# A one-core decoder layer with 32 experts: PSUM pairs released after the first reader, 1/rms by one-hot products, the last expert's weights in quarters

## Time and profile before

| | |
|---|---|
| runs shown | 824.47, 823.37, 822.83 us; median 823.37 |
| the profiled execution | 825.39 us, span 823.57 us |
| mean granted TensorE clock | 0.991 of full speed |
| busy | PE 721.8 us, DVE 288.8, ACT 179.6, POOL 102.6 |
| moved by DMA | 258.39 MB, mean 314 GB/s |

### The profile page before, as it was taken

One profiled execution on the slowest core, in us unless ns is written; L12 is line 12 of the kernel. 1 busy time (PEld: TensorE's weight loads), 2 busy tenths in 40 slices (PEclk: granted clock), 3 DMA queues, 4 the chain that ended last, 5 costly groups with the idle time before them and its releaser, 6 DMA issues.

```text
span 823.6 us, 11299 instructions
## 1 busy us (share of the span) xinstructions
PE 721.8 (88%) x4520; PEld 450.1 (55%) x4520; DVE 288.8 (35%) x520; ACT 179.6 (22%) x274; POOL 102.6 (12%) x161
## 2 busy tenths in 40 slices
PE   8999999999999888999998887777777777778996
PEld 8989999899998433333333222222222222226775
DVE  5556788676434532010111011011001001005875
ACT  7242312233323010011111010000000000004576
POOL 0500000010001112212121211211211111100000
PEclk9999999999999999999999999999999999999999
DMA  9641225663936799999999999999999999995301
GB/s 347 239 181 53 77 80 210 248 224 98 400 132 217 259 409 416 428 426 425 426 425 426 424 427 427 426 425 428 428 424 429 426 427 426 425 422 218 120 27 77
DMA packets 36457, 258.39 MB, mean 314 GB/s; under 512 B 7905, under 2 KB 8465, under 8 KB 22841
## 3 DMA queue, kind: packets, MB, share of 16 engines
q1 hardware_dynamic: 27248, 237.17, 70.3%
q0 software_dynamic: 7072, 19.07, 6.2%
q10 hardware_dynamic: 2096, 1.56, 0.6%
HBM read 251.04 MB, written 15.14 MB: 323 GB/s over the span
## 4 chain that ended last, share of the span: by engine, by line
PE 53%; DMA 36%; DVE 6%; ACT 3%; issue 2%; SPq 0%; DVEq 0%; POOLq 0%; ACTq 0%
DMA arena<-in_w_exp 33%; PE ps L1560 23%; PE ps L1754 15%; PE ps L1771 5%; PE ps L1885 3%; PE ps L1603 1%; DMA region_q<-in_xt 1%; DVE xh L1423 1%; DVE region_u L1376 1%; DMA region_u<-h_rows,index 1%; DMA region_m<-y_rows 1%; PE ps L1568 1%; DMA y_rows<-region_v,both_cols 1%; PE ps L1762 1%; PE ps L1673 0%
## 5 line engine op out<-in xcount | busy, mean ns | idle before, releaser
L1754 PE MATMUL ps<-arena,region_u 128*64 128x512 f32 x960 | 218.3, 600 | 47.0 <-DMA arena<-in_w_exp 46.0
L1754 PEld LDWEIGHTS ps<-arena,region_u 128*64 128x64 f32 x960 | 66.9, 137 | 196.2 <-issue 124.2
L1372 DVE SCALAR_TENSOR_TENSOR region_u<-ps,small,region_u 128x256 f32<-128x256 f32 x32 | 15.5, 484 | 376.7 <-ACT region_u L858 376.7
L1560 PE MATMUL ps<-u_hi,w_hi 128*128 128x260 f32 x448 | 129.2, 288 | 5.1 <-issue 3.3
L1560 PE MATMUL ps<-u_lo,w_hi 128*128 128x260 f32 x448 | 127.4, 284 | 0.0
L1560 PE MATMUL ps<-u_hi,w_low 128*128 128x260 f32 x448 | 127.3, 284 | 0.0
L1771 PE MATMUL ps<-arena,region_u 128*64 128x512 f32 x480 | 109.6, 598 | 6.1 <-DMA arena<-in_w_exp 2.5
L1560 PEld LDWEIGHTS ps<-u_hi,w_hi 128*128 128x128 f32 x448 | 85.1, 190 | 7.0 <-issue 5.0
L1560 PEld LDWEIGHTS ps<-u_hi,w_low 128*128 128x128 f32 x448 | 85.2, 190 | 0.0
L1560 PEld LDWEIGHTS ps<-u_lo,w_hi 128*128 128x128 f32 x448 | 85.2, 190 | 0.0
L682 POOL DMA_INDIRECT y_rows<-region_v,both_cols x32 | 33.3, 1042 | 367.6 <-ACT region_v L862 367.6
(11 more groups left out here) (288 smaller groups left out, 857.6 us busy)
## 6 DMA issues: line engine op xcount, KB each, us to landing
arena<-in_w_exp SPq DMA_DIRECT2D x88, 2048.0 KB, 26.9
arena<-in_w_in SPq DMA_DIRECT2D x35, 512.0 KB, 4.0
region_q<-in_w_exp SPq DMA_DIRECT2D x24, 256.0 KB, 11.1
arena<-in_w_exp SPq DMA_DIRECT2D x8, 512.0 KB, 4.2
arena<-in_w_ple_gate SPq DMA_DIRECT2D x2, 2048.0 KB, 23.6
region_u<-in_xt SPq DMA_DIRECT2D x2, 1040.0 KB, 6.2
arena<-in_state_ret POOLq DMA_DIRECT2D x2, 1024.0 KB, 9.1
xh<-v_few POOLq DMA_DIRECT2D x1, 2048.0 KB, 9.0
```

Source lines behind the costliest of these rows:

```text
L1372: V.scalar_tensor_tensor(hs[b], ps[:, 2 + b, 256:512], rs[b], sg[b], ALU.mult, ALU.mult).then_inc(out_sem, 1)
L1560: last = mm(halves(out)[:, half, :], w[:, k, :], u[:, cols], start=(k == 0 and s == 0), stop=(k == KD - 1 and s == 2))
L1754: last = mm(ps[side * 64:side * 64 + 64, 2 + b, :], xv[:, k // 4, k % 4, :], rows(k % 4 * 2 + side), start=(k == 0), stop=(k == KD - 1))
```

## The change

Four things, in the order of the kernel.

1. *Head.* DVE counts a q or k job as read after its first operation; a new semaphore `rotated` counts the sums, and PE's sc, DVE's far product, `state_row`, the mask of q3 and ACT's reuse of `rot` wait for it. ot's pair is read by ACT in place of DVE, right before the squares.
2. *Router.* `h_rows` has rows of 512 words; 1/rms goes into its own `r_rows`, which ACT stores after the first two experts and which only the branch for overfull experts gathers. For the others a new job rs makes a table on chip: DVE multiplies `pick` with 1/rms (one operation on 128x320), ACT widens the row one-hots to float32 (128x640), PE does 20 float32 products, DVE copies 32 columns. `evac_rows` reads the table. 16 spins after tot become 6 after rs.
3. *Weights.* Spare 1: its first two pieces are issued after POOL's first memset of a gather tile, the other two after `h_rows`. Spare 2 is issued when POOL has issued the first gather. For the last pair of experts SP's loop is written out; units 94 and 95 come in four DMAs each, with a semaphore for each quarter, and PE waits for them one by one.
4. *Tail.* 52 spins for 48, and 8 more before u of turn 1; DVE's order as below.

```diff
-READERS = dict(... ot="D" ...)
+READERS = dict(... ot="A" ..., rs="D")
+    jobs += [("rk", 0), ("ix", 0), ("iy", 0), ("tot", 0), ("rs", 0)]
-SPIN_TAIL = 48
+SPIN_TAIL, SPIN_ROWS = 52, 8
-HR = 528
-SPIN = (28, 8, 16)
+RW = 16
+SPIN = (28, 8, 6)
@@ SP
+            sp.wait_ge(xg_cleared, 1)
+            for n in range(2):
+                load_spare(1, n)
             sp.wait_ge(h_stored, 16 * 2 * len(STORES))
-            for n in range(4):
+            for n in range(2, 4):
                 load_spare(1, n)
-            sp.wait_ge(xg_loaded[0], 16)
+            sp.wait_ge(pool_turn, 2)
             for n in range(8):
                 load_spare(2, n)
...
-            with sp.Fori(4, NE // 2) as i:
+            with sp.Fori(4, NE // 2 - 1) as i:
...
+            for j in range(6):
+                unit, slot = NE * 3 - 6 + j, PAIR_SLOTS[j]
+                sp.wait_ge(used[j % 3], NE - 2 + (j // 3 - 1))
+                if j < 4:
+                    load_unit(unit, slot)
+                for n in range(PIECES if j >= 4 else 0):
+                    at = slice(n * PIECE, n * PIECE + PIECE)
+                    sp.dma_start(ring[:, slot, at], a["w_exp"][unit][:, at]).then_inc(last_loaded[j - 4][n], 16)
@@ POOL: the wait for rstd_stored moves into the branch for overfull experts
@@ ACT
-                        act.wait_ge(dve_jobs, HEAD.done("D", ROTATED[turn - 2]))
+                        act.wait_ge(rotated, turn - 1)
...
+                elif kind == "ot":
+                    nc.scalar.activation(qk[:, 0:H, SEQ:T], b[:, 0:H * NB].rearrange("p (h n) -> p h n", h=H),
+                                         ACT.Copy).then_inc(act_jobs, 1)
+                    act.wait_ge(act_jobs, done)
+                    for h in range(H):
+                        nc.scalar.activation(qk[:, H + h, :], qk[:, h, :], ACT.Square).then_inc(o_squared, 1)
...
-            act.wait_ge(rows_ready, 1)
-            for half in range(2):
-                act.dma_start(h_full[:, :, half, 512:HR], rstd_rows[:, 0:4, :]).then_inc(rstd_stored, 16)
-                act.dma_start(h_few[:, half, 512:HR], rstd_rows[0:NB, 4, :]).then_inc(rstd_stored, 16)
+            act.wait_ge(hot_done, 1)
+            nc.scalar.activation(hot_32, row_hot, ACT.Copy).then_inc(hot_widened, 1)
@@ ACT, after pair_of_experts(0)
+            act.wait_ge(rows_ready, 1)
+            for half in range(2):
+                act.dma_start(r_full[:, :, half, :], rstd_rows[:, 0:4, :]).then_inc(rstd_stored, 16)
+                act.dma_start(r_end[:, half, :], rstd_rows[0:NB, 4, :]).then_inc(rstd_stored, 16)
@@ DVE, q and k
-                    link(V.tensor_tensor(dst..., halves(b), cos_t..., ALU.mult))
+                    V.tensor_tensor(dst..., halves(b), cos_t..., ALU.mult).then_inc(dve_jobs, 1)
                     link(V.tensor_tensor(r, r, sin_t, ALU.mult))
-                    V.tensor_tensor(dst, dst, r, ALU.add).then_inc(dve_jobs, 1)
+                    dve.wait_ge(dve_jobs, done)
+                    V.tensor_tensor(dst, dst, r, ALU.add).then_inc(rotated, 1)
@@ DVE, rk and rs
+                    V.tensor_tensor(rs_value..., pick, stats[:, 10:15]..., ALU.mult).then_inc(value_ready, 1)
+                elif kind == "rs":
+                    V.tensor_copy(rs_table, b[:, 0:NE]).then_inc(dve_jobs, 1)
-                V.tensor_copy(rs[b], xg[b][:, 512:513])
+                V.tensor_copy(rs[b], rg[:, 0:1] if over else rs_table[:, bass.ds(count - 1, 1)])
@@ DVE, tail
-            combine(1, 1)
             gained(0)
+            combine(1, 1)
             gained(1)
...
                 if n + 1 < NT:
                     gained(n + 1)
-                    if n + 2 < NT:
-                        combine(n + 2, 0)
+                    if n >= 2:
+                        gated("pb", n - 1)
+                    if n == 1:
+                        combine(3, 0)
                     low_rows(n + 1)
-                    if n + 2 < NT:
-                        combine(n + 2, 1)
+                    if n == 1:
+                        combine(3, 1)
+                    if n == 2:
+                        combine(4, 0)
+                        combine(4, 1)
+                else:
+                    gated("pb", n - 1)
...
                 if n + 1 < NT:
                     gate_rstd(n + 1)
-                    gated("pb", n)
@@ PE
+                    pe.wait_ge(rotated, 1 + max(ROTATED.index((x, c)) for x in "qk"))
...
+                elif kind == "rs":
+                    pe.wait_ge(value_ready, 1)
+                    pe.wait_ge(hot_widened, 1)
+                    last = placed(b[:, 0:NE], hot_32, rs_value)
+                    spin(b[:, 512:1024], SPIN[2])
...
+                    if isinstance(filled, list):
+                        pe.wait_ge(filled[k % 4], 16)
...
+                    if pieces:
+                        pe.wait_ge(pieces[q], 16)
...
+                    if turn == 1:
+                        spin(b, SPIN_ROWS)
```

More of the change, by code:

```diff
@@ L153, in build @@
     y_rows = nc.dram_tensor("y_rows", [2 * T, D], F32, kind="Internal").ap()
-    h_rows = nc.dram_tensor("h_rows", [2 * T, HR], F32, kind="Internal").ap()
+    h_rows = nc.dram_tensor("h_rows", [2 * T, 512], F32, kind="Internal").ap()
+    r_rows = nc.dram_tensor("r_rows", [2 * T, RW], F32, kind="Internal").ap()
     v_few = nc.dram_tensor("v_few", [1, NB * H * P], F32, kind="Internal").ap()
@@ L159, in build @@
     h_few = h_rows[2 * SEQ:2 * T, :].rearrange("(p n) c -> p n c", n=2)
+    r_full = r_rows[0:2 * SEQ, :].rearrange("(t p n) c -> p t n c", p=P, n=2)
+    r_end = r_rows[2 * SEQ:2 * T, :].rearrange("(p n) c -> p n c", n=2)
     y_tok = y_rows.rearrange("(t k) c -> t (k c)", k=2)
@@ L333, in build @@
         xg, xgT, hs, sg, hT = [], [], [], [], []
-        for lst, width in ((xg, HR), (xgT, 512), (sg, 256), (hs, 256), (hT, 256)):
+        for lst, width in ((xg, 512), (xgT, 512), (sg, 256), (hs, 256), (hT, 256)):
             for _ in range(2):
@@ L375, in build @@
             sem("silu_g"), sem("v_centred"), sem("s_centred"), sem("o_squared"), sem("ret_made"))
+        rotated = sem("rotated")
         head_rstd, r_few_stored, r_wide_loaded = sem("head_rstd"), sem("r_few_stored"), sem("r_wide_loaded")
@@ L407, in build @@
         out_stored = [sem(f"out_stored{i}") for i in range(2)]
+        last_loaded = [[sem(f"last_loaded{j}{n}") for n in range(PIECES)] for j in range(2)]
         gu_half = sem("gu_half")
@@ L666, in _, with start_gather @@
             nc.gpsimd.memset(xg[1], 0.0).then_inc(xg_cleared, 1)
-            pool.wait_ge(xg_cleared, 2)
+            nc.gpsimd.memset(rg, 1.0).then_inc(xg_cleared, 1)
+            pool.wait_ge(xg_cleared, 3)
             pool.wait_ge(h_stored, 16 * 2 * len(STORES))
-            pool.wait_ge(rstd_stored, 16 * 4)
             pool.wait_ge(index_done, 1)
-            def start_gather(b, at, loaded):
+            def start_gather(b, at, loaded, rows=False):
                 pool.sem_inc(pool_turn, 1)
-                pool.indirect_dma_start(out=xg[b], out_offset=None, in_=h_rows,
+                pool.indirect_dma_start(out=rg if rows else xg[b], out_offset=None, in_=r_rows if rows else h_rows,
                                         in_offset=bass.IndirectOffsetOnAxis(ap=at, axis=0),
@@ L794, in _ @@
                     nc.scalar.activation(ret_hi[:, c, :], mixT[:, CC + c, :], ACT.Copy).then_inc(mix_high, 1)
[L795 to L799, removed]
                 if kind == "wo":
@@ L1156, in state_row @@
             def state_row(n):
+                dve.wait_ge(rotated, 2 * H)
                 kcol = qk[:, H:2 * H, SEQ + n:SEQ + n + 1].to_broadcast([P, H, P])
@@ L1246, in _ @@
                     dve.wait_ge(half_copied, turn + 1)
-                    link(V.tensor_tensor(dst.rearrange(two, b=2), halves(b), cos_t.rearrange(two, b=2), ALU.mult))
+                    V.tensor_tensor(dst.rearrange(two, b=2), halves(b), cos_t.rearrange(two, b=2), ALU.mult).then_inc(dve_jobs, 1)
                     link(V.tensor_tensor(r, r, sin_t, ALU.mult))
-                    V.tensor_tensor(dst, dst, r, ALU.add).then_inc(dve_jobs, 1)
+                    dve.wait_ge(dve_jobs, done)
+                    V.tensor_tensor(dst, dst, r, ALU.add).then_inc(rotated, 1)
                     if (kind, c) == ("q", H - 1):
-                        dve.wait_ge(dve_jobs, done)
+                        dve.wait_ge(rotated, turn + 1)
                         link(V.memset(q_mask, 0.0))
@@ L1270, in _ @@
                         link(V.tensor_tensor(w_r, w_r, wide(col["gffn"], [P, KD, NR]), ALU.mult))
+                    dve.wait_ge(rotated, 1 + max(ROTATED.index((x, c)) for x in "qk"))
                     link(V.tensor_tensor(q_far, qk[:, c, P:SEQ], far[:, c, :], ALU.mult))
@@ L1378, in _, with evac_rows @@
             gx = col["gx"].rearrange("p (k h) -> p k h", h=2).unsqueeze(3).to_broadcast([P, 4, 2, ROWS])
-            def evac_rows(b, count, t_done, out_sem):
```

(18 more changed lines are left out.)

32 lines of the change are left out of this document (18 added, 14 removed).

## The result

The changed kernel takes 817.4 us (median of 6 runs, 815.56 to 819.58) against 823.9 for the kernel before, beside it; the ratio is 0.9927 (95% interval 0.9910 to 0.9945). That is a gain of 6.0 us (4.5 to 7.4) where 10.2 were forecast. The sign and the range held (817.6 was its upper end), the likeliest case (811.5 to 815) did not. A second set of six runs gave 818.2, just outside that range, and 0.9938 (0.9917 to 0.9958).

What follows compares the result with a forecast made beforehand. PE bounds to about 260 us and from 761, full DMA engines from about 285 to 753. Parts 5.7 + 2.2 - 0.2 + 2.5 = 10.2 us take the median from 823.4 to 813.2; range 809.8 to 817.6.

Steps and rivals of the forecast that it cites:

- Part 1, head: PE's waits before k1, k2, k3 2.8 us, clock after the long wait 1.6, vs 1.3: 5.7 us gained (4.0 to 6.2).
- Rival E: The head's saving is absorbed by a late weight load: 818 us; chance 0.03.
- Part 2, router and stream: Expert 0 starts 1.3 us sooner and weight units are issued sooner, less small store and gather costs: 2.2 us (0 to 3.5).
- rs ends near 274.1, the weights near 277.3: Router: after 2.1 us of float32 products, DVE's routing weights set expert 0's start near 278.2, 1.3 us sooner.
- with the queue emptier than in either I take 3.4: Router: the first gather, issued as before, lands after 3.4 us in place of 5.1, at 276.2.
- Rival B: Router: rs or Exp comes so late that expert 0 starts as before and the stream gains nothing: 815.4; chance 0.15.
- Part 3, quarters: Last expert: scatter issued 3.5 us sooner but hidden behind the gate weights; extra DMAs cost 0.2: -0.2 us (-0.8 to 2.8).
- Rival A: Last scatter isn't hidden, gets through near 748, y loads follow behind the gate weights: 2.8 us more, 810.4; chance 0.15.
- Part 4, tail: pa1 starts 1.2 us sooner by spins before u1, and pa3's wait of 1.3 goes: 2.5 us (0 to 3).
- Rival C: Half clock moves into the tail, the eight spins take 3.6 us instead of 1.8: 815; chance 0.15.
- Rival D: Small packets or h_rows' row pitch slow each pair of experts; over 0.7 us per pair loses the gain; chance 0.05.
- the prediction's later case for Exp: Router: a table load of about 2.66 us after the hot copy ends Exp near 274.6, costing part 2 0.3 us.

Runs made afterwards that it cites:

- both moved: The change with spare 2's pieces behind the gather's issue and DVE's routing weights ahead of the rs copy: 815.02 us; also without quarters, with 48 tail spins: 814.75.
- tail_only: The kernel before with the tail's part alone (52 spins, 8 before u of turn 1, DVE's new order): 822.64 us, ratio 0.9992.
- router_spare: The kernel before with the router's part and the order of the spares alone: 827.13 us, ratio 1.0050.
- before_again: The kernel before, unchanged, measured once more for a second profile: 823.65 us, ratio 1.0006.
- head_only: The kernel before with the head's part alone (q and k pairs back after the first operation, ot on ACT): 817.7 us, ratio 0.9932.

## Why the prediction was right or wrong

**Part 1, head: right.** 5.7 forecast (4.0 to 6.2), 5.6 by the ratio. The terms were shifted against each other. By the starts of the chunks k2 and k3 bring 1.1 us each, not 0.5 and 0.8: the idle time in a list of waits leaves out what a wait adds between two starts. Against that, the 1.6 us of clock in k1 belongs to 2 of 7 executions, hardly to the median. Rival E (the saving is absorbed) is out: the last split begins 5.4 us sooner in the mean.

**Part 2, router and stream: wrong.** The failed step is "rs ends near 274.1, the weights near 277.3", with "I take 2.1" for the 20 float32 products. They took 3.7 us (from the increment of tot at 268.0 to the copy at 271.7), near the upper bound of 4.3, so the weights end 7.2 us behind the index and not 5.9, and expert 0 cannot begin before 8.1. The step beside it, "with the queue emptier than in either I take 3.4", failed as well: spare 2's first piece goes out 0.2 us ahead of the gather, and the gather takes 5.4 us; with the pieces behind it, the first transpose came 3.3 to 3.7 us behind its issue, and 4.5 to 6.8 with them ahead. So expert 0 begins 8.5 us behind the index in place of 8.15, where 6.9 was forecast. That is where part 2 was lost. From expert 0's start to the first y load the seven kernels with the change's order take 472.9 us in the mean, the eight of before 473.6, so 0.8 less; the prediction has 0.9 for this stretch, 2.2 less the 1.3 of the start. In sum 0.4 us by profiles for 2.2. On top of head, tail and quarters the router's part is worth 0.2 to 1.1 by the ratios; alone it loses. The edits show the two bounds: with both moved, expert 0 begins at 6.6. The time is then 1.4 to 2.6 us less by the ratios, near what part 2 was to bring, but that this comes from the sooner start alone is not shown, as said above. Rival B (the router's side jobs bind) named the mechanism, with 0.15, and gave 815.4 for it. The step that ruled it out was the product's price taken from a row of other products.

**Part 3, quarters: hidden, as forecast, with one step wrong.** The scatter was to go out 3.5 us sooner and went out 1.3 sooner. The forecast let PE meet the last quarter of unit 94 with 4 products left. But PE starts on the half before it only when unit 93 lands, at 727.0, and the 32 products of both halves take 7.1 us in one go, to 734.2; the last quarter of unit 94 had landed at 732.1. So PE's own products bound silu, and no longer the loads. That made no difference to the sum, since the scatter was hidden: it took 6.3 us for 4.4, and the y load came 0.6 later. Rival A (not hidden) is out: it landed at 747.75, 0.2 us behind the gate weights. By the page "DMA: Bandwidth & Descriptors" of the Trainium skill (Queues, rings and completion order) a small transfer would wait for one share and go; the trace has 6.3 us, less than the 8 of a full queue and more than the 4.4 of an idle one, so it did not go at once. The price of 0.2 fits the 0.3 inside the change and is too low for the 0.6 of the profiles and for the other kernels (2 to 3).

**Part 4, tail: sizes right in the profile, not in the median.** 1.1 + 1.55 us for 1.2 + 1.3 in the profile. By the ratios 0.7 alone (with 52 spins) and 1.4 on top of the head (with 48). In 4 of the 14 profiles with the new tail pa1 came 0.9 to 1.5 us later than in the others: once u0 waited for the spins (tail_only), three times the second y load landed 6.4 to 6.7 us behind the first one's issue in place of 5.3. Rival C (half clock moves into the tail) is out: no profile with the 8 spins has 0.50 near u1.

**Rival D** (the stream's pace) is out as a whole: from the landing of the 21st ring unit behind expert 0's start to that of the 76th it takes 287.0 to 287.6 us in all twenty profiles.

**The sum** was made on one profiled execution. Its own 1.6 us of clock loss in k1 was booked as gain, and two profiles of before lay 2 to 3 us above the median of their runs. The table load, 1.28 us long again and now behind the hot copy, had no effect: the ACTIVATE began 1.29 us behind the load's start, so the prediction's later case for Exp did not come either, and Exp ended 2.5 us before the weights began.

What stays open: why router and quarters cost 3 to 4 us when put alone into the kernel before and 0 to 2 on top of head and tail. Apart from stretches at half clock, which cost 1.5 us in the router and, in router_spare, some 2 in the tail, their profiles show 1 us at most. And the stage means of the profiles add up to some 2 us more than the measured gain. Of the 4.2 us between 10.2 and 6.0, part 2 explains 1.8 by the profiles. Of the rest, the largest piece that can be named is the tail's: 2.6 us in the profiles, 0.7 to 1.4 in the times.

## What to carry to other kernels

When an operation is put in front of another on an engine that runs in order, the price is the arrival of its input, not its own length: put the copy of a side result behind the work that the path needs. When a load is moved forward, look what small, urgent transfer is issued right behind it, and let that go first. When a load is cut in pieces, count from the last point where the engine behind it was free: here PE had 7.1 us of products left, and only 1.3 of the 3.5 us could come. And take the forecast's base from what several executions share: a stretch at half clock in the one profile is neither a cost nor a gain of the code until it shows in a second.

## What the hardware showed that was not expected

- 20 float32 products of 64 columns of weights by 32 moved columns took 3.7 us until the reader was released, though their rows in the trace end 2.3 us behind their start (2.31 us for x40); six spins behind them, or none, made no difference (the copy came 4.07 to 4.18 us behind the index with them, 4.17 without).
- The rows of a gather of 128 half rows were being transposed 3.3 to 3.7 us behind its issue with eight pieces of 256 KB issued behind it, 4.5 to 6.8 us with them issued 0.2 us ahead. With the order of before it was 3.5 us where the last of four pieces had gone out 5.1 us ahead of it (before_again) and 7.0 where it had gone out 1.5 us ahead (head_only).
- The same code meets 1.2 GHz in one execution and not in the next, in stretches of 3.4 or 6.8 us, behind the same short pauses of PE.
